# A mixer on one core: weights turned by products with diagonals, and the output product begun between the last rounds

## What is computed

```python
def hybrid_layer(x, ...):                       # second stage, after its first SwiGLU
    h = rms_norm(x, mix_pre_g)
    proj = h @ w_in
    q, k, v, z, xbc, dt = jnp.split(proj, IN_SPLITS, axis=-1)
    attn = diff_attention(q, k, v, lam, attn_subln_g, lambda_init).astype(x.dtype)
    ssm = ssd_mixer(z, xbc, dt, conv_w, conv_b, dt_bias, a_log, d_skip, ssm_norm_g)
    mixed = jnp.concatenate([attn, ssm], axis=-1) @ w_out      # 512 + 1024 rows, 1024 columns
    x = x + rms_norm(mixed, mix_post_g)
...
        a = probs(q1b, k1) - lam * probs(q2b, k2)              # 8 heads
        return jnp.einsum('bhqk,bhkv->bhqv', a, v)
    o = rms_norm(o, subln_g) * (1.0 - lambda_init)
```

## Time and profile before

| | us |
|---|---|
| median of 3 runs (1244.6 to 1252.46) | 1248.87 |
| the profiled execution | 1247.42 |
| its span in the profile | 1245.6 |
| rounds 0 to 12, from the first states product to the first product of `mo` | 944.63 to 1002.19 |
| `mo` | 1002.19 to 1038.99 |
| until `gate2` is in full run | 1058.37 |
| PE busy of the span | 1193.1 (96%) |
| DVE busy of the span | 835.6 (67%) |

### The profile page before, as it was taken

One profiled execution on the slowest core, in us unless ns is written; L12 is line 12 of the kernel. 1 busy time (PEld: TensorE's weight loads), 2 busy tenths in 40 slices (PEclk: granted clock), 3 DMA queues, 4 the chain that ended last, 5 costly groups with the idle time before them and its releaser, 6 DMA issues.

```text
span 1245.6 us, 19087 instructions
## 1 busy us (share of the span) xinstructions
PE 1193.1 (96%) x7698; PEld 1041.5 (84%) x7698; DVE 835.6 (67%) x1291; ACT 652.7 (52%) x1060; POOL 236.3 (19%) x300
## 2 busy tenths in 40 slices
PE   6898999999999999999999999999998799999996
PEld 6786788888888688888888889999996489888996
DVE  5966776666586586666667766457865867777643
ACT  6427666643343666664446555336545545656532
POOL 4104422110000341120012221000005510121101
PEclk9999999999999999999999999999999789999998
DMA  7790254555453334556543554653441033555451
GB/s 278 258 231 35 82 189 173 199 203 200 142 201 154 152 135 171 202 181 225 188 182 144 197 182 146 208 210 106 169 176 52 1 115 131 197 179 200 151 199 57
DMA packets 34088, 205.56 MB, mean 165 GB/s; under 512 B 3776, under 2 KB 6352, under 8 KB 13776
## 3 DMA queue, kind: packets, MB, share of 16 engines
q1 hardware_dynamic: 30704, 200.47, 45.0%
q10 hardware_dynamic: 3296, 3.87, 1.5%
HBM read 202.87 MB, written 1.46 MB: 164 GB/s over the span
## 4 chain that ended last, share of the span: by engine, by line
PE 79%; DVE 14%; ACT 4%; POOL 1%; issue 1%; DMA 0%; POOLq 0%; ACTq 0%; DVEq 0%
PE ps L662 37%; PE ps L667 23%; PE ps L665 5%; PE ps L666 5%; DVE wl L604 3%; PE ps L686 1%; PE ps L687 1%; PE ps L688 1%; DVE tf L2189 1%; DVE y L1940 1%; DVE xb L740 1%; ACT wh L575 1%; ACT pb L917 1%; DMA h<-xt 0%; ACT pb L916 0%
## 5 line engine op out<-in xcount | busy, mean ns | idle before, releaser
L604 DVE TENSOR_TENSOR wl<-raw,wh 128x2048 fp32r<-128x2048 f32 (+4 forms) x196 | 421.1, 2154 | 145.2 <-ACT wh L575 145.1
L662 PE MATMUL ps<-xb,wh 128*128 128x512 f32 x1424 | 500.9, 398 | 4.4 <-DVE wl L604 3.8
L667 PE MATMUL ps<-xb,wl 128*128 128x256 f32 x1696 | 475.9, 281 | 0.0
L575 ACT ACTIVATE wh<-raw 128x2048 fp32r<-128x2048 f32 (+4 forms) x196 | 348.6, 1781 | 148.0 <-PE ps L667 111.6
L662 PEld LDWEIGHTS ps<-xb,wh 128*128 128x128 f32 x1424 | 267.6, 188 | 70.3 <-issue 5.5
L667 PEld LDWEIGHTS ps<-xb,wl 128*128 128x128 f32 x1696 | 322.0, 190 | 0.0
L667 PE MATMUL ps<-ab,wl 128*128 128x256 f32 x1088 | 306.4, 282 | 0.0
L662 PE MATMUL ps<-ab,wh 128*128 128x512 f32 x640 | 225.4, 398 | 0.2
L667 PEld LDWEIGHTS ps<-ab,wl 128*128 128x128 f32 x1088 | 207.7, 191 | 0.0
L662 PEld LDWEIGHTS ps<-ab,wh 128*128 128x128 f32 x640 | 120.2, 188 | 29.8 <-DVE ab L975 0.8
L859 DVE TENSOR_TENSOR tf<-ps,tf 128x256 f32<-128x256 f32 x148 | 61.8, 421 | 118.3 <-ACT tf L854 118.1
(11 more groups left out here) (322 smaller groups left out, 1324.7 us busy)
## 6 DMA issues: line engine op xcount, KB each, us to landing
raw<-wstream SPq DMA_DIRECT2D x156, 1024.0 KB, 4.8
raw<-wstream SPq DMA_DIRECT2D x32, 704.0 KB, 4.1
raw<-wstream SPq DMA_DIRECT2D x8, 768.0 KB, 4.1
e_bt<-scratch ACTq DMA_DIRECT2D x16, 128.0 KB, 8.1
o_bt<-scratch SPq DMA_DIRECT2D x2, 1024.0 KB, 9.8
raw<-wstream SPq DMA_DIRECT2D x2, 560.0 KB, 7.4
raw<-wstream SPq DMA_DIRECT2D x4, 256.0 KB, 6.5
h<-xt ACTq DMA_DIRECT2D x4, 256.0 KB, 7.7
```

The source lines that it names most:

```text
L575: e.g.activation(WH[i % HLN][:, 0:w], RAW[i % RAWN][:, 0:w], ACT.Copy).then_inc(S["hi"], 1)
L604: e.g.tensor_tensor(WL[q][:, 0:w], RAW[i % RAWN][:, 0:w], f32(WH[q][:, 0:w]), ALU.subtract).then_inc(S["lo"], 1)
L662: e.g.matmul(PS[b][:, :].rearrange("p (a t) -> p a t", a=2), wh[:, sl], x2[:, :, cs], start=start, stop=k == p.nk - 1, skip_group_check=pair)
L667: ins = e.g.matmul(o, wl[:, sl], xh[:, cs], start=False, stop=k == p.nk - 1, skip_group_check=pair)
```

## The change

**Weights and their order.** The first four output tiles of `w_out` come tile by tile of the input (k outside, n inside), the others as before, all in chunks of 16 blocks: 6 chunks of 2048 columns for 8 of 1536. `mo` gets fixed banks 3, 4, 0, 1, 2, and `gate2` begins in 5 and 6 (before: 3 and 4); `pe_idle` takes its bank from there.

**Turn.** The combined tile is no longer made. POOL and ACT each write two 128 x 128 diagonals (identity times the factor of a row) into the new `m_d`, and PE forms each third of the turned tile as two products, one for each job, added in PSUM.

**Order.** POOL weighs two rounds ahead. DVE does the reciprocals and `skipped` before the late steps. The epsilon is added by ACT out of PSUM (`first_factor`), and DVE's two additions go. PE does a `sub` sum behind the states instead of ahead of the decay.

**`mo` begun.** From round 7 on PE multiplies the ready tiles by the first four output tiles between the rounds' work (`begun`). The third chunk is rounded by ACT in round 0 and by DVE in quarters in rounds 1 to 4, the fourth by ACT in round 10 and by DVE in rounds 11 and 12.

```diff
-    cols("w_out_2", 0, tiles(0, 8), MIXK, 12)
+    half = [("w_out_2", 0, k * 128, n * 128, 128) for k in MIXK for n in range(4)]
+    half += [("w_out_2", 0, k * 128, n * 128, 128) for n in range(4, 8) for k in MIXK]
+    for i in range(0, len(half), 16):
+        chunks.append(half[i:i + 16])
...
-        Gemm("mo", "cols", 8, 12, 12, "pg"),
-        Gemm("gate2", "cols", 2 * F2, 8, 16, "ev_dve", kmajor=4, after=6, fixed=(3, 4), wide=True),
+        Gemm("mo", "cols", 8, 12, 16, "pg", kmajor=4, fixed=(3, 4, 0, 1, 2)),
+        Gemm("gate2", "cols", 2 * F2, 8, 16, "ev_dve", kmajor=4, after=6, fixed=(5, 6, 0, 1, 2, 3, 4), wide=True),
...
+            def first_factor(e, no, a, o):
+
+                e.wait_ge(S["nb_m"], no)
+                e.wait_ge(S["eps"], 1)
+                e.link(e.g.activation(o, PS[NB][:, 0:T], ACT.Ln, bias=EPS[:, 1:2]))
+                e.g.activation(a, PS[NB][:, 0:T], ACT.Identity, bias=EPS[:, 1:2]).then_inc(S["nb_a"], 1)
+                e.settle()
+                e.g.activation(o, o, ACT.Exp, scale=-0.5).then_inc(S["nb_y"], 1)
...
                 if 0 <= i - 1 < 8:
                     act_turned(e, A, 2 * (i - 1) + 1)
+                if i < 8:
+                    e.wait_ge(S["iw"], i + 1)
+                    if i >= 2:
+                        e.wait_ge(S["tp"], A.pv_base + i - 1)
+                    for tb, d in enumerate(diagonal(i, 1)):
+                        ins = e.g.activation(d, c_("ident"), ACT.Copy, scale=rs(2 * i + 1)[:, tb:tb + 1])
+                    ins.then_inc(S["dga"], 1)
...
                 if i + 2 < 8:
                     act_decay(e, i + 2)
+                if i == 0:
+                    hi_to(e, G["mo"].first + 2)
...
+                if i == 10:
+                    hi_to(e, G["mo"].first + 3)
...
             weighted(0)
+            weighted(1)
             gated(0)
             A = MIX
             for i in range(ROUNDS):
-                if i + 1 < 8:
-                    weighted(i + 1)
                 if i < 8:
-                    p, r = PB[2 * i % 4], rs(2 * i)
                     e.wait_ge(S["iv"], A.base + i + 1)
-                    for tb, s in ((0, slice(0, 128)), (1, slice(128, 384))):
-                        ins = e.g.tensor_scalar(p[:, s], p[:, s], r[:, tb:tb + 1], 1.0, ALU.mult, ALU.mult)
-                    ins.then_inc(S["fw"], 1)
+                    if i >= 2:
+                        e.wait_ge(S["tp"], A.pv_base + i - 1)
+                    for tb, d in enumerate(diagonal(i, 0)):
+                        ins = e.g.tensor_scalar(d, c_("ident"), rs(2 * i)[:, tb:tb + 1], 1.0, ALU.mult, ALU.mult)
+                    ins.then_inc(S["dgp"], 1)
+                if i + 2 < 8:
+                    weighted(i + 2)
                 if i + 1 < 8:
                     gated(i + 1)
...
+                if 1 <= i <= 4:
+                    lo_part(e, G["mo"].first + 2, i - 1)
+                if i >= 11:
+                    lo_part(e, G["mo"].first + 3, 2 * i - 22)
+                    lo_part(e, G["mo"].first + 3, 2 * i - 21)
...
-                if i < 8:
-                    p, r, first = PB[(j + 1) % 4], rs(j + 1), PB[j % 4]
-                    e.wait_ge(S["fw"], i + 1)
-                    for tb, s in ((0, slice(0, 128)), (1, slice(128, 384))):
-                        ins = e.g.scalar_tensor_tensor(out=p[:, s], in0=p[:, s], scalar=r[:, tb:tb + 1], in1=first[:, s],
-                                                       op0=ALU.mult, op1=ALU.add)
-                    ins.then_inc(S["wt"], 1)
...
+            def begun(*tiles):
+
+                for t in tiles:
+                    at = 4 * MIXK.index(t)
+                    pe_cols(e, G["mo"], MIXK, AB, ready, part=slice(at, at + 4))
+
...
+                if i == 7:
+                    begun(4)
                 if i % 2 and 0 <= i - 3 < 8:
                     pe_mixer_pv(e, (i - 3) // 2)
                 if i % 4 == 3 and i < 8:
                     e.wait_ge(S["gq"], i + 1)
                     pe_sums(e, "ones512", (ACC, ACC2)[i // 4][:, :], nb_no("grp", i // 4))
-
-            def ready(e, k):
-                e.wait_ge(S["ml"], mixed_no(k))
-
-            pe_cols(e, G["mo"], MIXK, AB, ready)
+                begun(*{7: (5, 0), 8: (6, 7), 9: (1,), 10: (8, 9), 11: (2,), 12: (10, 11, 3)}.get(i, ()))
+            pe_cols(e, G["mo"], MIXK, AB, ready, part=slice(48, None))
...
-            e.wait_ge(S["wt"], A.base + h + 1)
+            e.wait_ge(S["dgp"], h + 1)
+            e.wait_ge(S["dga"], h + 1)
...
-                ins = e.g.transpose(PS[b][:, s], PB[(2 * h + 1) % 4][:, s], c_("ident"))
+                for job in range(2):
+                    ins = e.g.matmul(PS[b][:, s], PB[(2 * h + job) % 4][:, s], diagonal(h, job)[x > 0], start=job == 0,
+                                     stop=job == 1)
```

More of the change, by code:

```diff
@@ L240, in __init__ @@
                 order += [(n, k, n // 2, 2 * k + n if name == "r" else n % 2 * nk + k) for k in range(nk) for n in range(n0)]
+            elif kmajor:
+                n0 = kmajor
+                order += [(n, k, (k * n0 + n) // per, (k * n0 + n) % per) for k in range(nk) for n in range(n0)]
             elif per == nk:
@@ L501, in build @@
         m_oa = place("m_oa", 4 * T, at=xs_at)
+        m_d = [place(f"m_d{i}", 512, at=xs_at) for i in range(2)]
         m_xdt = [place(f"m_xdt{i}", D, at=[o + 8192, o + 12288]) for i, o in enumerate((ah_at, al_at))]
@@ L1988, in pe_idle @@
             wh, _ = pe_chunk(e, p.first + p.chunks)
-            o = PS[3]
-            e.wait(G["mu" if at == 0 else "gate2"].free[0])
+            to = G["mu" if at == 0 else "gate2"]
+            o = PS[to.bank[0]]
+            e.wait(to.free[0])
             for i in range(36):
@@ L2023, in eb, with diagonal @@
             return m_eb[2 * (p % 2) + x]
+        def diagonal(i, x):
+            return [m_d[i % 2][:, 256 * x + 128 * tb:256 * x + 128 * tb + 128] for tb in range(2)]
         def cbt(h):
@@ L2111, in act_mixer @@
                     act_turned(e, A, 2 * (i - 1) + 1)
+                if i < 8:
[5 more added lines that the diff above has]
+                    ins.then_inc(S["dga"], 1)
+                for kind, s, step in late_steps(i):
+                    if (kind, step) == ("grp", 1):
+                        if s:
+                            e.wait_ge(S["yn"], 4 * s)
+                        first_factor(e, nb_no("grp", s), TMP[1][:, 0:T], RB[:, 0:T])
                 if i + 2 < 8:
                     act_decay(e, i + 2)
+                if i == 0:
+                    hi_to(e, G["mo"].first + 2)
                 s = (i - 3) // 2
@@ L2280, in dve_mixer @@
                     weighted(i + 1)
+                if i < 8:
+                    j = 2 * i
+                    e.wait_ge(S["ex"], A.base + j + 1)
+                    e.g.reciprocal(rs(j), sm(j)).then_inc(S["iv"], 1)
+                    e.wait_ge(S["ex"], A.base + j + 2)
+                    e.link(e.g.reciprocal(rs(j + 1), sm(j + 1)))
+                    e.settle()
+                    e.g.tensor_scalar(rs(j + 1), rs(j + 1), LAM[:, 2:3], None, ALU.mult).then_inc(S["iw"], 1)
+                if i + 1 < 8:
+                    skipped(i + 1)
                 for kind, s, step in late_steps(i):
-                    if kind == "sub" and step == 2:
-                        e.wait_ge(S["nb_m"], nb_no("sub", s))
-                        e.g.tensor_scalar(RT[:, 0:T], PS[NB][:, 0:T], 1e-6, None, ALU.add).then_inc(S["nb_a"], 1)
-                    elif kind == "sub" and step == 3:
+                    if kind == "sub" and step == 3:
                         oa = m_oa[:, tile(s)]
@@ L2294, in dve_mixer @@
                         mixed_low(e, s, m_oa[:, tile(s)])
-                    elif kind == "grp" and step == 1:
-                        e.wait_ge(S["nb_m"], nb_no("grp", s))
-                        e.g.tensor_scalar(TMP[1][:, 0:T], PS[NB][:, 0:T], 1e-6, None, ALU.add).then_inc(S["nb_a"], 1)
                     elif kind == "grp":
-                        if step == 2:
+                        if step == 1:
                             e.wait_ge(S["nb_y"], nb_no("grp", s))
@@ L2365, in pe_mixer, with ready @@
             pe_states(e, 0)
+            def ready(e, k):
+                e.wait_ge(S["ml"], mixed_no(k))
+            def begun(*tiles):
+                for t in tiles:
+                    at = 4 * MIXK.index(t)
+                    pe_cols(e, G["mo"], MIXK, AB, ready, part=slice(at, at + 4))
             A = MIX
@@ L2371, in pe_mixer @@
                     pe_mixer_turn(e, i - 1)
+                if i + 2 < 8:
+                    pe_decay(e, i + 2)
+                if i + 1 < 8:
+                    pe_states(e, i + 1)
                 for kind, s, step in late_steps(i):
```

29 lines of the change are left out of this document (6 added, 23 removed).

## The result

The changed kernel takes 1244.89 us (median of 12 runs, 1238.43 to 1246.73) against 1249.88 us before (12 runs): a ratio of 0.9950, 95% interval 0.9933 to 0.9968. That is 5 us faster: clear of the noise, but under the one per cent (12.5 us) that the prediction took as the border of "no change", and 8 us above the 1237 that was forecast; the range ended at 1244. In two later sets of runs, both on one chip, the ratio was 0.9941 (0.9922 to 0.9960) and 0.9951 (0.9936 to 0.9966).

A forecast was written before the change was run, and what follows sets the result against it. The prediction took POOL's 5.23 us weighing loop as the pace, with DVE late in round 6. 4.6 us up to head 7's scores plus 6.8 to the end of `mo` made 11.4 gained: 1237 us, range 1231 to 1244.

The forecast's parts named there:

- The turn: Turning a tile on PE by six fp32 products: 1.3 us against 0.30 for three transposes, diagonals ready in time.
- POOL's circle: Round 1's loop through POOL's weighing, PE's states, DVE's `skipped` and POOL's gating, 5.23 us; weighing two ahead opens it.
- ScalarE's 1.9 us in round 0: ACT's `hi_to` of `mo` weights in round 0 delays round 1's exponentials by about 1.5 us; 0.6 stays.
- S7 to end: From the start of head 7's scores on PE to the end of `mo`: 44.1 us against 50.9, 6.8 us gained.
- the 1.3 us stall before tiles 8 and 9: After the last turn PE waits 1.3 us for ACT's and DVE's norm steps and low parts; the one stall seen.
- the 19.5 us behind `mo`: The stretch behind the output product, 19.4 us in the prediction, stays as it was and costs nothing.
- Norm steps: ACT adds the epsilon, 0.35 us more there and less on DVE; rounds 4 to 6 forecast at 5.7, 5.8, 5.1 us.
- DVE's lateness: In round 5 DVE's late work runs to 14.3 us, while head 6's scores are there at 13.0: 1.3 us late.
- This supposes full clock all through.: Assumption behind the 44.1 us from the start of head 7's scores to the end of `mo`: PE's clock never falls.
- the clock falls all the same: Rival: PE's clock falls in round 6 anyway, 5 us lost, 1242 to 1243, or 1248 if long; chance 0.12.
- DVE or ACT set the rounds: Rival: these engines, not PE, pace the seven rounds, 0.7 us over in each, 5 us lost, 1242 to 1244; chance 0.12.

The follow-up runs named there:

- the filled gap: The changed kernel with 22 spare 128-column products put into TensorE's wait ahead of the last states in round 6: 1243.4 us, ratio 0.9939.

## Why the prediction failed

**Right.** The turn: twelve records in 1.3 us, with no wait for a diagonal. Opening POOL's circle: rounds 1 and 2 at 5.7 and 5.0 us, 5.6 and 5.0 forecast. ScalarE's 1.9 us in round 0: 0.7 us on the path (5.71 against 4.98 without it), 0.6 forecast. The begun products: at full clock S7 to end is 43.6 (the filled gap), 44.1 forecast. That this is so near is partly luck: the 1.3 us stall before tiles 8 and 9 did not come, and the 1.40 us for bank 6 came instead, ahead of them. Nothing happened in the 19.5 us behind `mo`.

**The step that failed** is in *Norm steps*: "The exponentials of round 6 end at 16.3, so S7 is 5.1 us after S6 and not PE's 4.2." It follows DVE's lateness only through the exponentials to the scores. But ahead of the scores of head 7 PE has the last states, and these wait for DVE's weighing, which stands behind the maxima, which stand behind the late steps. Two things made that long. I had the lateness at 1.3 us with steps of 0.42 each; it was 2.1, as POOL stretched them to 1.11, 0.84 and 0.72. The order is the larger part: even with two of the three at 0.43 and 0.48, PE waited 1.86 us. The earlier trace rows had shown one of 1.21, and I had used it for a rival only. And I had asked of each engine when it is free, not what else its queue holds back. Round 6 was 7.29 us, or 7.8, instead of 5.1.

**From it followed the second:** "This supposes full clock all through." The gap of 2.55 us brought some 7 us at half clock, 2.8 to 3.1 us on the path. In two of three profiles there were another 3.5 us at half clock in round 5, which made that round 1.2 us longer; these stand ahead of the failed step and did not come from it. I had given "the clock falls all the same" a chance of its own, as if it were independent of "DVE or ACT set the rounds". Behind S7 it was the consequence. Together they end near 1244, where each alone was put at 1242 to 1244.

**The third** is a term left out: bank 6. With ScalarE reading the sums, the next sum waits until ScalarE comes to it in its own order, in round 4 behind the diagonals (0.95 us) and in round 8 behind the turned tile (1.40). I had cost the norm steps on ACT and DVE and not asked who wants the bank next. The figures for it stood in the prediction: ScalarE's first factor from 5.3 to 6.5 us after S4, where PE's work of a round is 5.05; and in the tail ACT's copy and first factor behind the turn that ends at 10.0, where the sum was put at 10.0 to 10.7 without a wait. The trace of before showed the wait as well, 1.70 us in round 4.

In numbers, the stretch after against forecast, 87.6 to 82.2: round 4 +0.9, round 5 +0.2, round 6 +2.2, tail +2.3, the first four rounds -0.3. The tail is +2.8 for the clock, +1.4 for the bank, -1.3 for the stall that stayed away, and -0.6 for the rest. With the late steps and the first factors moved, the stretch is 82.2.

One reading of before was short: the prediction has the clock low for 22 us there; by its rows it is some 24.

The rule of the Trainium skill, TensorE: Matmul & The Clock Gate, Terms, that the transpose mode is 4 times faster for fp32, was weighed against a row saying twice; the turn's twelve records in 1.26 us, 0.21 per product against 0.10 per transpose, agree with the row, a factor of 2, and not with a factor of 4.

## What to carry to other kernels

When an engine is late, walk down the whole queue of the engine that waits: the first instruction in it that wants something from the late engine counts, not the one that the argument is about. A gap and the clock are one event: where the forecast leaves a gap of the size behind which the trace already showed half clock, price the two together. And where the reading of a PSUM bank moves to another engine, ask at once when that engine's order lets it read, and who writes the bank next.
